# Products of the identity ahead of six waits of TensorE in the tail of pass 1's last tile

## The reference, cut to what matters

```
h    = modulate(rms_norm(x, norm1_g), sh1, sc1)
proj = h @ w_in
feat = feat + (prev - feat) * shift_mix          # group A (RWKV-7): token shift
w    = -softplus(-(w0 + tanh(w_lo) @ w2)) - 0.5  # decay
iclr = sigmoid(a0 + a_lo @ a2);  gate = sigmoid(g_lo) @ g2
kk   = k * k_k / norm(k * k_k);  k = k * (1 + (iclr - 1) * k_a)
# group B: attention over this chunk of 64 and the one before, with a sink
probs = softmax(concat(q k^T / 8 + bias, sink));  out = probs v
```

## Time and profile before

| what | value |
|---|---|
| median of 3 runs | 2655.66 us (2652.34 to 2657.85) |
| the profiled execution's own time | 2654.44 us |
| its span, first to last instruction | 2652.6 us |
| TensorE busy | 2392.2 us, 90% |
| VectorE, ScalarE, GpSimd busy | 1096.3, 752.1, 389.9 us |
| mean granted clock of TensorE | 0.959 |

### The profile page before, as it was taken

The page is one execution under the profiler, slowest core; times in us unless marked ns, Lnnn a source line. Parts: engine busy times, 40 slices in busy tenths (PEclk is TensorE's granted clock), DMA queues, the critical chain, the costliest instruction groups (busy, mean ns, idle before and its releaser), DMA issues. The chain is left out here.

```text
span 2652.6 us, 67742 instructions
## 1 busy us (share of the span) xinstructions
PE 2392.2 (90%) x27916; PEld 1467.1 (55%) x27917; DVE 1096.3 (41%) x2600; ACT 752.1 (28%) x1847; POOL 389.9 (15%) x480
## 2 busy tenths in 40 slices
PE   6999999999996899999999997799999999999960
PEld 4787787877765677777776764332333323232220
DVE  1456565555654355555656556111111111111118
ACT  1444535445442123232222321121222212221212
POOL 1111211211111122121212210010110101010000
PEclk9999999999997899999999998799999999999985
DMA  9021211112118422222222221934535596999959
GB/s 341 19 87 49 96 49 74 72 49 96 49 80 329 166 84 90 106 90 106 74 104 84 90 74 74 422 142 193 219 137 231 195 373 242 386 384 389 388 219 365
DMA packets 54245, 451.81 MB, mean 170 GB/s; under 512 B 7884, under 2 KB 8944, under 8 KB 32528
## 3 DMA queue, kind: packets, MB, share of 16 engines
q1 hardware_dynamic: 37656, 391.24, 37.7%
q0 software_dynamic: 10656, 38.80, 3.8%
q10 hardware_dynamic: 5720, 18.66, 1.8%
HBM read 367.41 MB, written 87.56 MB: 172 GB/s over the span
## 5 line engine op out<-in xcount | busy, mean ns | idle before, releaser
L1816 PE MATMUL ps<-arena 128*32 128x512 f32 x4608 | 510.6, 600 | 27.1 <-DMA arena<-wex 18.9
L452 PE MATMUL ps<-arena 128*128 128x128 f32 x3072 | 354.1, 276 | 14.7 <-ACT arena L598 14.7
L452 PEld LDWEIGHTS ps<-arena 128*128 128x128 f32 x3072 | 348.5, 192 | 27.3 <-ACT arena L598 24.5
L1816 PEld LDWEIGHTS ps<-arena 128*32 128x32 f32 x4608 | 149.8, 111 | 381.1 <-issue 366.5
L1126 PE MATMUL ps<-arena 64*64 64x64 f32 x8704 | 297.7, 222 | 29.3 <-ACT arena L1355 9.5
L1126 PEld LDWEIGHTS ps<-arena 64*64 64x64 f32 x8704 | 277.4, 136 | 58.6 <-issue 57.8
L1830 PE MATMUL ps<-arena 128*32 128x512 f32 x2304 | 264.7, 600 | 10.4 <-DMA arena<-wex 10.1
L1271 PE MATMUL ps<-arena 128*128 128x512 f32 x480 | 222.0, 605 | 0.0
L2043 DVE TENSOR_TENSOR arena<-arena,ps 128x256 f32<-128x256 f32 x72 | 29.9, 415 | 463.6 <-ACT arena L1874 463.6
L467 PE MATMUL ps<-arena 128*128 128x512 f32 (+1 forms) x512 | 213.9, 555 | 0.0
L1874 ACT ACT_TABLE_LOAD x36 | 46.2, 1283 | 583.5 <-PE ps L1816 583.5
(11 more groups left out here) (345 smaller groups left out, 2882.4 us busy)
## 6 DMA issues: line engine op xcount, KB each, us to landing
arena<-wex SPq DMA_DIRECT2D x105, 2048.0 KB
mid<-arena SPq DMA_DIRECT2D x16, 2568.0 KB, 8.5
arena<-mid SPq DMA_DIRECT2D x16, 2568.0 KB, 9.8
arena<-ada SPq DMA_DIRECT2D x12, 2048.0 KB, 9.5
arena<-y SPq DMA_DIRECT2D x16, 1024.0 KB, 7.9
arena<-x SPq DMA_DIRECT2D x31, 512.0 KB, 5.8
arena<-x ACTq DMA_DIRECT2D x17, 512.0 KB, 10.6
arena<-w_in SPq DMA_DIRECT2D x4, 2048.0 KB, 39.1
```

Source lines behind the costliest of these rows:

```text
L452: mm = pe.matmul(bank[name][:, at:at + P], V["w_in"][g][:, kk, at:at + P], V["hT"][:, kk, :], start=(kk == 0), stop=(kk == KD - 1))
L1816: mm = pe.matmul(bank[("HA", "HB")[g]][rows[j], :], xT[:, kk, rows[j]], slot[j][:, at:at + 2 * FH], start=(kk == 0), stop=(kk == KD - 1))
```

## The change

In the last tile alone (t = 15), six steps of TensorE get products of the identity ahead of their waits: 3 ahead of `nbc`, 3 ahead of `att2`, 5 ahead of `att3_0`, 13 ahead of `tok1`, and 2 each ahead of `att4_0` and `att4_1`; 28 in all. They go to bank A1, behind a wait until `kv` of the last tile has been copied out of it.

```
+    def fill_wait(pe, t, n):
+        if isinstance(t, int) and t == nt - 1:
+            B.wait_read(pe, "A1", "kv", t)
+            idle_products(pe, bank["A1"], ident, n)
...
             def nbc(t, b):
+                fill_wait(pe, t, 3)
                 S.wait(pe, "sq", t + 1)
...
             def tok(uses):
                 def go(t, b):
+                    if uses[0][0] == "tokA":
+                        fill_wait(pe, t, 13)
                     S.wait(pe, "ew3", t + 1)
...
             def att2(t, b):
+                fill_wait(pe, t, 3)
                 S.wait(pe, "qn", t + 1)
...
             def att3(g):
                 def go(t, b):
+                    if g == 0:
+                        fill_wait(pe, t, 5)
                     B.wait_read(pe, "T0", "qT", t)
...
             def att4(g):
                 def go(t, b):
+                    fill_wait(pe, t, 2)
                     S.wait(pe, "probs", 2 * t + g + 1)
```

## The result

The changed kernel takes 2661.42 us (median of 11 runs, 2658.39 to 2667.33) against 2654.45 for the kernel before in the same rounds (11 runs, 2647.94 to 2659.93). The ratio is 1.0028, with a 95% interval of 1.0018 to 1.0038: some 7 us slower. The profiled execution took 2658.60 us. Ratios leave out three slow executions of the last group of runs: 2703.92 us of the kernel with 28 tiny products, 2883.97 and 4898.42 us of the kernel before.

A forecast was written before the change was run, and what follows sets the result against it. Pass 1's tail was taken as bound by engines waiting on each other, not by TensorE, up to L870's end. Tail +3.7 and pass 2's head −1.0 gave +2.7 us, forecast 2658.3 us, range 2654 to 2662.8.

The forecast's parts named there:

- rival 1: Last tile of pass 1: the clock falls under the added product groups themselves; +5.4 to +7.1 us, 2661 to 2663; chance 0.15.
- rival 2: Behind L513's start: the clock falls again because transposes follow the fill; +5.0 us, 2660.7; chance 0.05.
- Fill of 0.43 us a record: Added products in the last tile: each record takes 0.43 us at the upper clock, a product 0.86 us.
- L513 5.0 late: Behind the 13 products at `tok1`: 26 records end at 812.4, operands there at 807.39, so TensorE comes 5.0 us late.
- Tail +3.7: End of pass 1: 5.0 us late at L513 less 1.3 us regained after it, so last work ends 3.7 us later.
- rival 5: Tail of pass 1: the products do not act on the clock; +27 us or more, 2683; chance 0.03.
- L501: Behind the first 3 products: starts 0.6 us late, hidden, with over 3 us of cover before its reader.
- L530: Behind the second 3 products: on time and some 0.7 us shorter, but nothing taken for it.
- −1.0 at L1113: Head of pass 2: first half of 64 products takes about 1.05 us at the upper clock, not 2.1; −1.0 us.
- the 0 taken there: Head of pass 2, 128 products of L1126: no gain taken, as VectorE's gaps stay; −1.7 us as the bound.
- Rival 3: Pass 2's first tiles: the clock stays up; 2650, chance 0.05, and 0.15 for a sum between −1 and +1.7.
- Rival 4: Added code, 112 instructions: a stop like the 1.98 us one may come or go; 2656 or 2660; chance 0.12.

The follow-up runs named there:

- the kernel with the fitted fill: Changed kernel with its wide products cut to 2, 2, 3, 5, 0, 0 and 52 tiny ones, 256 instructions added; ratio to the kernel before 0.9987.

## Why the prediction was right and wrong

The time, 2661.42, lies in the range of 2654.0 to 2662.8, near its upper end, and that is in part luck. The change measured 0.28%, and to slower by over 0.2% I gave 0.25; my sum of +2.7 us was less than half of the measured 7. The range had been widened for rivals that did not come (1 and 2), and for a stop of ±2 us.

*The tail: right.* Fill of 0.43 us a record: 26 records in 11.43 us. L513 5.0 late: 5.14. Tail +3.7: +3.87. The four profiles with this tail start pass 2 at 37.55 or 37.56; those with the tail of before lie at 33.00 to 34.78, so the +3.87 against one of them is good to about 1 us. The clock held through the fill and through the transposes behind it (1.00 from 784 to 827.3), so rivals 1, 2 and 5 are out; the Trainium skill's remark on transposes, in "TensorE: Matmul & The Clock Gate", Part 4, finds no support in this trace either, since L521 ran at the upper clock with its 16 transposes (1.04 us for 8). The rise at 811.3 in the earlier trace rows is the stronger row; in the kernel with the fitted fill the clock fell at 806.1, behind 54 records of tiny products and the first 8 transposes, and that trace does not decide between the page and the rise. L501 came 0.6 us late and nothing was gained or lost by it or by L530, as forecast.

*The head of pass 2: right as far as it went.* −1.0 at L1113: −0.88 (3.87 to 2.99). The 128 products behind it fell into a dip again (834.1 to 837.5), so the 0 taken there held too: 5.62 us against 5.53.

*Rival 3: there in part, and too small.* In the profile the clock was up for more of pass 2's head: 0.95 from 828 to 932 us, against 0.88 from 825 to 928 before. The changed kernel is 7.0 us late at the second mod product and 2.7 us late at 925, so some of the 4.3 us between may be the clock's; the timed runs show no gain from it.

*The added code: the step that failed.* Rival 4 had the mechanism, with ±2 us and a chance of 0.12, and the sum had nothing for it. It is a term of the sum, of about +4 us: in the profile the stops are 5.5 us instead of 2.0 and the second mod product 7.0 us late with 3.0 of it from the tail; in time, 28 tiny products against 64 are 4.5 us. Tail and head 3.0 plus code 4.2 to 4.5 is 7.2 to 7.5, and 1.0028 is 7.4. That the two terms add up is not shown by a run of its own: the two kernels with the change and a whole block, which should keep the 3.0 alone, give 1.0027 and 1.0014, the first with a cost of its own and the second with new stops. I had the stop of 1.98 us in my rows and left its cause open, taking it for equally likely to come or to go. Counting records to it and to the 0.20 us with `<-issue` at 837.52, 512 records ahead of it and in the trace though not in my rows, would have pointed to block borders, and to 112 instructions earlier as their new places, in the middle of dense products. How long TensorE would stand there could not have been read from it.

The Trainium skill, "Runtime: NRT & Kernel Launch", section "Instruction fetch mechanics", says that code is refilled in 16 KiB blocks of 256 instructions, and that a sequencer fetches the next block while it executes the present one, so that fetching is hidden, or mostly so. The size is what the stops' distance and the packets show. That it is hidden, these traces contradict: 1.7 to 8 us of stops in some 30 us of pass 2's head.

*What stays open.* Why some borders stop TensorE and others don't (the run with 36 tiny products in the setup). The stops do not end with the head either: from 870 to 1650 us, past pass 2's end, all further ones over 0.3 us stand at block borders too. They sum to 8.20 us before and 5.38 after, so over the whole pass it is 10.2 against 10.8 us. In these two profiles the changed kernel's larger stops in the head are nearly made up for by smaller ones later. That the code costs 4 us in time rests on the timed pairs alone. And the profiles do not carry the whole 7 us to the end: in the changed kernel's, the last instruction comes 0.9 us later than before, counted from tile 15's first product, with 6 us of the 7 regained in places after 870 us, partly at those later stops, partly where before the clock was low and now is not. The dips fall differently in each execution; one profile of each cannot tell their average, and the 11 runs of each say that on average it is not regained.

## What to carry to other kernels

Idle products held the clock here, but on an engine that works in order they must end before the data comes: size each group to its own wait, here at 0.86 us a product, and put none where a wait is only just there. That a fill so sized wins time is not shown. Instructions that cost almost no time on the engine still move the code: 112 ahead of a dense stretch of small products made 0.08 to 0.15% here, and filling up to a whole block of 256 took it back in two pairs of kernels. So compare an edit to TensorE's program with one that adds the same count of instructions and does nothing, before its time is read as the work's.

## What the runs showed of the hardware

TensorE's code arrives in blocks of 256 instructions, 16 KB each, and at every stop in the head of pass 2 TensorE goes on 1.2 to 1.5 us after the packet has landed. Stops of 0.85 to 4.02 us came at the same three instructions in every kernel with the same count ahead of them (45564, 45308, 45052 records to the end with 112 added, in eight profiles of seven kernels). They came with the DMA engines full and at a share of 0.12. An increment of a counter on TensorE took 0.15 us: 16 more of them in a row (72 for 56) made 2.45 us. A tiny product, four instructions, took 0.12 us (26 records, 13 products, in 1.54 us). And the clock: it went to 0.50 at 806.4 us, during the 26 narrow records of 4 columns (0.15 us each) ahead of L531; in the changed kernel, with 26 records of 512 columns in their place, it stayed at 1.00.
